# Hybrid streaming encoder step: two gate tiles move from the attention steps' fillers to a thirteenth block-product pair

## The chip, the cores and the metric

One NeuronCore of a Trainium2 chip runs the whole program. The metric is the device time of one execution in microseconds (us), taken as the median of several executions.

Engines are named as in the profile: PE is TensorE (matrix products; PEld its weight loads), DVE is VectorE, ACT is ScalarE, POOL is GpSimd, SP is the queue that issues most DMAs. Each of them runs its own program in order, and waits on semaphores that the others raise.

## What is computed

One layer of a streaming encoder, for 1024 prompt tokens and 32 sample tokens, in float32:

```python
z = x @ w_in                       # 1024 x 6416: heads of all branches, and gl, the 3 x 1024 merge gates
A: GLA linear attention            # 4 heads, per-token recurrence, in blocks
B: sliding-window attention        # 8 query heads, 2 kv heads, with sinks and partial rotary
C: cross attention                 # 4 heads into 256 memory tokens
mix = (sig(g_a)*y_a + sig(g_b)*y_b + sig(g_c)*y_c) @ w_o
x = LN1(alpha*x + mix);  x = LN2(alpha*x + ConvFFN(x))
```

The change concerns only where some columns of `gl` (the gates' part of `x @ w_in`) are computed. `gl` has 3072 columns, that is 24 tiles of 128.

## The kernel before

**Precision.** Every float32 product is made of three matmuls: operands are split into a high part (ACT copies it, rounded) and a low part (DVE subtracts it from the original), and hi x hi, hi x lo, lo x hi are accumulated (`product`, L1277).

**Dense tiles.** 128 columns of a weight are one tile. All 1058 token columns are passed in three slices (`GROUPS`, 352, 352 and 354 wide), each with 8 row blocks of 128, so a tile is 24 units of three matmuls. A slice is evacuated by ACT, and a gate tile's slices are stored in the scratch tensor `gates` by SP.

**Block-product pairs.** In the first long stage the columns are made two tiles at a time by a 2 x 2 block scheme with seven products in place of eight (`z_product`, L1302, `z_pair`, L1340): 7 products x 4 row blocks x 3 matmuls, for two halves of the tokens (256 and 274 wide), that is 168 matmuls for a pair. There are `NZ = 12` pairs: seven for the scan branch's columns, five for gate tiles, which `Z_GATES` names by the first of two. While PE works on pair n, ACT and DVE split the weights of pair n+1, snapshot and combine the results (`z_window`, L2083 on ACT, L2778 on DVE), and SP loads weights and stores the two tiles (`z_load`, `z_keep`). Raw weights, result buffers and PSUM banks alternate by the parity of the pair. Pairs 0 and 1 are written out, pairs 2 to 9 are a loop of four turns, 10 and 11 are written out again (L1418 to L1422). POOL makes sums of other weights in this stage.

**Scan stage.** The GLA recurrence, nine tiles of tokens; PE's gaps are filled with 14 dense tiles.

**Attention steps.** Then 8 token tiles are taken in 24 steps, three for each (window attention for kv pair 0 and 1, then memory attention), and three more short ones for the sample tokens. The order is written out by hand on each engine. PE, in step k = 6i + j (`att_steps`, L1667):

1. fillers: `ATT_UNITS = 6` units of a dense gate tile (`gate_slice_b`, L1651); the first three steps have other work in their place
2. `turn_probs(k)`, L1596: 8 transposes of the probabilities into PSUM
3. `scores(k+2)`, L1576 or L1581
4. `values(k)`, L1608 or L1613: needs prob_T, the transposed probabilities, copied back by DVE (one half) and ACT (the other)

DVE, in the same step (`att_steps`, L3005): its copy of prob_T(k) (L2980), `normalise(k+1)` (L2963: sum, reciprocal, four scalings L2974), `max_unit(k+2)` (L2939: mask add L2947, row maximum L2952, bias L2954; for memory units only the maximum L2959 and the bias L2961). In steps with j = 1 or 4 the copy of prob_T stands behind `normalise`. ACT (`att_steps`, L2291): an evacuation of a filler slice when one ends, its copy of prob_T(k) (L2236), the copy of the values (L2245), a split of the next weights when a tile ends, and `exp_unit(k+2)` (L2220), which waits for the bias from DVE; `normalise(k+2)` on DVE waits for it. Scores use the same PSUM banks each time, so `scores_read` (L1617) makes PE wait until they have been read. POOL copies the next token tile's operands when a memory unit's scores are made (`att_stage`, L1140).

With 24 units to a tile and six to a step, 24 steps (21 full ones and the three of the sample tokens) make six gate tiles, numbers 16 to 21, from turn `T_GATE_B`. In the sample steps (`r` = 0, 1, 2; from L1698 on PE, L2320 on ACT) ACT also makes the high parts of the branch outputs (`branch_hi`, L2317) for the merge stage, which begins with L1279 on `o_hi`.

**Queues and counts.** `gate_loop` (L845, SP) loads and stores the tiles of the attention steps; `load` waits until the slot's last weights were split. `T_MERGE`, `T_WO` and `T_FFN` number the weight tiles that follow, `PS_END` counts dense slices, `W0` counts loads.

Of the kernel before, what the change touches and what calls it, by code (L numbers as in the profile page):

```python
# [27 lines left out]
SEQ, DEC = 1024, 32  # L28
# [5 lines left out]
NT = SEQ // P  # L34
# [13 lines left out]
Z_BASE = (0, TT - 2 * HALF[1])  # L48
Z_FIRST = (0, 3, 1, 2, 5, 4, 6)
Z_SUMS = (1, 2, 4, 6)  # L50
NZ = 12
Z_LAST = (NZ - 1) % 2
ZA, ZS, ZC = NZ * 7, NZ * 4, NZ * 3
A_KEEP, Z_KEEP = 24, 34
FILL_ROWS = (0, 1, 8, 9, 2, 3, 4, 5)
NFILL = 14
FILL_SLICES = (5, 5, 5, 5, 5, 5, 4, 4, 4)
Z_GATES = (12, 14, 6, 8, 22)
ATT_UNITS = 6
H = 4  # L60
RANK = 16
GA_ROWS = 6 * RANK + 2
# [20 lines left out]
T_MQ = T_FILL + NFILL  # L83
# [1 line left out]
T_MQ_B = T_MQ + 3  # L85
T_MV = T_MQ + 6
T_GATE_B = T_MQ + 10
T_MERGE = T_MQ + 16
T_WO = T_MQ + 28
T_FFN = T_MQ + 36  # L90


PW0, PW1, PBG, PW2, PCB, PGN, PHI = 0, NF * 2, NF * 4, NF * 4 + 24, NF * 6 + 24, NF * 8 + 24, NF * 8 + 25
# [121 lines left out]
def program(nc, I, O, ctx):  # L215
# [114 lines left out]
    gate_st2 = [a.take(f"gate_stb{i}", [P, GW], F32) for i in range(3)]  # L330
# [175 lines left out]

    BRANCHES = (2, 0, 1)

    PS_Z, PS_G, PS_GA, PS_FILL, PS_MQ, PS_MQ_B, PS_MK, PS_MV, PS_GATE_B, PS_END = 6, 9, 11, 15, 57, 60, 63, 65, 67, 85
    q = Semaphores(sem)  # L510
    w_landed = [sem(f"w_landed{i}") for i in range(2)]
    x_landed = [sem(f"x_landed{i}") for i in range(6)]
    gate_stored = [sem(f"gate_stored{i}") for i in range(3)]
# [66 lines left out]
    LAST = NF - 1  # L580
# [4 lines left out]
    XH0, XL0, XS0 = 26, 17, 8  # L585
    HH0, HL0, XT0 = XH0 + len(X_ORDER), XL0 + len(X_ORDER), XS0 + 8
    D0 = T_FFN
    W0 = T_WO // 2 + 7
    KEPT = 16 * 9

    def mix_bank(p):
# [12 lines left out]
    def raw_count(c, par):  # L604

        if par:
            return 448 if isinstance(c, int) and c < 2 else c * 32 + 416
        return 32 * (W0 + 1) if isinstance(c, int) and c < 2 else c * 16 + 32 * (W0 + 1)

# [17 lines left out]
    d_landed = [w_landed[0], w_landed[1], h_landed[0], h_landed[1], rot_landed[0], rot_landed[1]]  # L627
    D_BASE = (32 * (W0 + NF // 2), 32 * (W0 + NF // 2), 0, 0, 16 * 8, 16 * 25)
    b_landed = [raw_b_landed, gate_landed[0], gate_landed[1], gate_stored[0], gate_stored[1], gate_stored[2]]
    B_BASE = (raw_count(LAST, 1), 192, 192, 16 * (8 + NFILL), 16 * (8 + NFILL), 16 * (8 + NFILL))  # L630
    B_RAWS = (1, 2, 1, 2, 1, 0, 0, 1, 1)

    def d_of(n):
# [56 lines left out]
    def _(sp):  # L690
# [154 lines left out]
        def gate_loop(turn0, chunk0, n, staging, stored0):  # L845

            for j in range(2):
                cols(turn0, j, w_in, C_GL + (chunk0 + j) * P)
            def stores(i, slots=(0, 1)):
                for j in slots:  # L850
                    for s, (c, w) in enumerate(GROUPS):

                        sp.wait_ge(q.proj_free, stored0 + i * 6 + 3 * j + s + 1)
                        sp.dma_start(gates[bass.ds(i * 2 + chunk0 + j, 1), :, c:c + w].rearrange("a p c -> p (a c)"),
                                     staging[s][:, 0:w]).then_inc(gate_stored[s], 16)
            with sp.Fori(0, n - 1) as i:
                for j in range(2):
                    cols(i + (turn0 + 1), j, w_in, i * 256 + C_GL + (chunk0 + 2 + j) * P)
                stores(i)
            return stores  # L860
# [36 lines left out]
        sp.dma_start(mask_first[:, :], I["c_mask_first"]).then_inc(q.params, 16)  # L897
        for n_ in range(4, 8):
            mem_tile(n_)
        last = gate_loop(T_GATE_B // 2, 16, 3, gate_st2, PS_GATE_B)  # L900


        def merge_tile(turn, slot, br, mp):
# [20 lines left out]

        merge_tile(T_MERGE // 2, 0, BRANCHES[0], 0)
        merge_tile(T_MERGE // 2, 1, BRANCHES[1], 0)
        last(2, (0,))
        sp.wait_ge(q.staged, 2 * NT + 2)
        sp.wait_ge(q.sample_turned, 1)
        gate_back(0)  # L930
        last(2, (1,))
        for s in range(3):
            sp.wait_ge(gate_stored[s], 16 * (8 + NFILL))

        for k in range(12):
            if k == 11:
# [339 lines left out]
    def _(pe):  # L1276
# [63 lines left out]
        def z_pair(n, par, j0=0):  # L1340
            for j in range(j0, NA):
                for s in range(2):
                    z_product(n, par, s, j)
# [71 lines left out]
        z_product(0, 0, 1, 6)  # L1415
        z_product(1, 1, 1, 0)
        z_pair(1, 1, 1)
        with pe.Fori(1, (NZ - 1) // 2) as i:  # L1418
            z_pair(i * 2, 0)
            z_pair(i * 2 + 1, 1)  # L1420
        z_pair(NZ - 2, 0)
        z_pair(NZ - 1, Z_LAST)  # L1422

        tile_start(1, 0)
# [165 lines left out]
        def turn_probs(k, par, w, widths):  # L1590
            pe.wait_ge(q.prob_ready, k + 1)
            pe.wait_ge(q.pT_dve, k)
            pe.wait_ge(q.pT_act, k)
            for h in range(H):
                for s, n in enumerate(widths):
                    last = pe.transpose(pair8(4)[0:n, 2 * h + s, 0:w], prob[par][0:w, h, s * P:s * P + n], ident[0:w, 0:w])  # L1596
            last.then_inc(q.prob_turned, 1)
# [53 lines left out]
        def gate_slice_b(i, j, beside=None):  # L1651

            for n_, (s, k) in enumerate(att_units(i, j)):
                slot, (c, w) = s // 3 % 2, GROUPS[s % 3]
                out = bank((PS_GATE_B + s) % 2)[:, 0:w]
                if k == 0:
                    if s % 3 == 0:
                        tile_start((T_GATE_B + s // 3) // 2, slot)
                    pe.wait_ge(q.proj_free, PS_GATE_B + s - 1)
                last = product(out, w_hi[slot][:, k, :], w_lo[slot][:, k, :], act_hi[:, k, c:c + w], act_lo[:, k, c:c + w],  # L1660
                               k == 0, k == KD - 1)
                if k == KD - 1:
                    last.then_inc(q.proj_done, 1)
                if beside and n_ in beside:
                    beside[n_]()
# [32 lines left out]
        for r in range(3):  # L1698
            k, widths = 3 * NT + r, (P, DEC) if r < 2 else (P, P)
            if r == 0:  # L1700
                gate_slice_b(NT // 2, r)
                turn_probs(k, k % 2, DEC, widths)
                sample_scores(2)
            else:
                gate_slice_b(NT // 2, r, {3: lambda: turn_probs(k, k % 2, DEC, widths)})
            pe.wait_ge(q.vt_ready, NT + 1)
            values(k, r, DEC, (v_hist, vt[0]) if r < 2 else mv[1], widths)

# [243 lines left out]
    def _(act):  # L1952
        def split_hi(turn, slot, dst=None, used=None):


            if used is not None:
                act.wait_ge(*used)
            act.wait_ge(w_landed[slot], 32 if isinstance(turn, int) and turn == 0 else (turn + 7) * 32)
            dst = w_hi[slot] if dst is None else dst
            act.activation(dst[:, :, :], w_raw[slot][:, :, :], ACT.Copy).then_inc(q.w_split_hi, 1)  # L1960

# [121 lines left out]
        def z_window(n, par):  # L2083
            for k in range(3):
                for s in range(2):
                    z_snap(n, par, s, k)
                z_split(n + 1, 1 - par, k)
            for j in (3, 4, 5):
                z_split(n + 1, 1 - par, j)
            for s in range(2):  # L2090
                z_snap(n, par, s, 3)
            z_split(n + 1, 1 - par, 6)

        z_window(1, 1)
        with act.Fori(1, (NZ - 1) // 2) as i:
            z_window(i * 2, 0)
            z_window(i * 2 + 1, 1)
        z_window(NZ - 2, 0)
        for k in range(3):
            for s in range(2):  # L2100
                z_snap(NZ - 1, Z_LAST, s, k)
# [23 lines left out]
        for gi, (c, w) in enumerate(GROUPS):  # L2125
            s = PS_GA + gi
# [232 lines left out]
        act.wait_ge(q.st_memv, 16)  # L2359
        act.wait_ge(q.v_out_ready, 1)  # L2360
        for gi in range(3):
            act.wait_ge(gate_stored[gi], 16 * (8 + NFILL))
        act.wait_ge(q.k_turned, 1)
        for place in range(3, 6):
            branch_hi(place)
# [300 lines left out]
    def _(dve):  # L2666
# [125 lines left out]
            z_low(n + 1, 1 - par, 6)  # L2792

        z_window(1, 1)
        with dve.Fori(1, (NZ - 1) // 2) as i:
            z_window(i * 2, 0)
            z_window(i * 2 + 1, 1)
        z_window(NZ - 2, 0)
        for k in range(3):
            for s in range(2):  # L2800
                z_combine(NZ - 1, Z_LAST, s, k)
# [681 lines left out]
```

## Time and profile before

| | us |
|---|---|
| median of 3 runs | 1712.73 (1712.61 to 1715.02) |
| the profiled execution, its own time | 1714.32 |
| its span, first to last instruction | 1712.5 |
| PE busy | 1689.7 (99%) |
| DVE busy | 1154.3 (67%) |
| ACT busy | 775.7 (45%) |
| POOL busy | 307.0 (18%) |

The stages by the timeline: block pairs from 42 to 291 us of the span, the scan stage to about 538, the memory keys and values and the first attention steps to 603, attention steps with fillers to 745, sample steps to 759, merging to about 906, output projection and layer norm to about 1010, the feed-forward to the end. A busy share is a mean over stages: whether an engine bounds a stage is read from its windows, waits and order of instructions.

### The profile page before, as it was taken

What the parts mean: (1) busy time and instruction counts of PE and PEld (TensorE: products, weight loads), DVE (VectorE), ACT (ScalarE), POOL (GpSimd) and SP (SyncE); (2) the same over time, 40 slices, a digit from 0 to 9 for tenths busy, and PEclk for the clock granted to TensorE, in tenths of its full rate; (3) what the DMA queues carried; (4) which work ended last, traced back from release to release, by engine and by line L of the source; (5) the groups of instructions that cost most, each with busy time, mean ns of one, the idle gap of its engine ahead of it and who ended that gap; (6) DMA issues with size and microseconds to landing.
All of it is one profiled execution on the core that took longest, in us unless ns stands there. A gap on an engine that the chain in (4) does not pass through costs nothing.

```text
span 1712.5 us, 32762 instructions
## 1 busy us (share of the span) xinstructions
PE 1689.7 (99%) x12447; PEld 1633.1 (95%) x12447; DVE 1154.3 (67%) x1687; ACT 775.7 (45%) x1500; POOL 307.0 (18%) x398
## 2 busy tenths in 40 slices
PE   9999999999999999999999999999999999999997
PEld 9999999999999889889997889999999999999997
DVE  6756553456673777667656698777777777777676
ACT  6433332354453555563332155455445445544562
POOL 0144342000010110000000004333333332000022
PEclk9999999999999999999999999999999999999999
DMA  5565665822154521124456332222222222787633
GB/s 169 162 223 199 211 216 169 278 76 76 59 166 126 170 81 47 43 65 150 137 177 218 108 96 79 75 74 74 75 82 85 80 74 88 271 302 247 207 102 100
DMA packets 196314, 232.75 MB, mean 136 GB/s; under 512 B 21973, under 2 KB 145430, under 8 KB 196214
## 3 DMA queue, kind: packets, MB, share of 16 engines
q1 hardware_dynamic: 188006, 201.66, 37.7%
q0 software_dynamic: 8208, 29.72, 4.8%
q8 instruction: 67, 1.10, 0.3%
q14 instruction: 33, 0.27, 0.0%
HBM read 170.69 MB, written 60.07 MB: 135 GB/s over the span
## 4 chain that ended last, share of the span: by engine, by line
PE 62%; DVE 5%; ACT 2%; issue 1%; POOL 0%; DMA 0%; DVEq 0%; ACTq 0%; POOLq 0%
PE banks L1836 24%; PE banks L1891 13%; PE banks L1279 5%; PE banks L1281 5%; PE banks L1280 5%; PE banks L1769 4%; PE banks L1596 1%; PE banks L1608 1%; PE banks L1613 1%; PE banks L1576 1%; ACT prob L2225 1%; PE banks L1581 1%; DVE prob L2974 1%; DVE wo L3050 0%; PE banks L1867 0%
## 5 line engine op out<-in xcount | busy, mean ns | idle before, releaser
L1836 PE MATMUL banks<-x_free_r,a_hi 128*128 128x256 f32 x1232 | 226.7, 282 | 2.0 <-DVE a_lo L3161 1.6
L1279 PE MATMUL banks<-act_hi,w_hi 128*128 128x352 f32 (+1 forms) x608 | 202.9, 334 | 0.0
L1281 PE MATMUL banks<-act_hi,w_lo 128*128 128x352 f32 (+1 forms) x608 | 197.8, 325 | 0.0
L1280 PE MATMUL banks<-act_lo,w_hi 128*128 128x352 f32 (+1 forms) x608 | 197.7, 325 | 0.0
L1836 PEld LDWEIGHTS banks<-x_free_r,a_hi 128*128 128x128 f32 x1232 | 190.1, 188 | 2.7 <-issue 1.2
L1836 PE MATMUL banks<-xs_hi,a_hi 128*128 128x274 f32 x616 | 178.8, 290 | 1.6 <-DVE xs_lo L3187 0.9
L1836 PE MATMUL banks<-xs_lo,a_hi 128*128 128x274 f32 x616 | 178.4, 290 | 0.0
L1836 PE MATMUL banks<-xs_hi,a_lo 128*128 128x274 f32 x616 | 178.3, 289 | 0.0
L1891 PE MATMUL banks<-b_hi,d_hi 128*128 128x238 f32 (+1 forms) x616 | 177.5, 288 | 0.4 <-DVE b_lo L3317 0.3
L1891 PE MATMUL banks<-b_hi,d_lo 128*128 128x238 f32 (+1 forms) x616 | 176.6, 287 | 0.0
L1891 PE MATMUL banks<-b_lo,d_hi 128*128 128x238 f32 (+1 forms) x616 | 176.4, 286 | 0.0
L1836 PE MATMUL banks<-x_free_r,a_lo 128*128 128x256 f32 x616 | 173.4, 281 | 0.0
L1836 PEld LDWEIGHTS banks<-xs_hi,a_hi 128*128 128x128 f32 x616 | 116.4, 189 | 2.2 <-DVE xs_lo L3187 1.4
L1891 PEld LDWEIGHTS banks<-b_hi,d_hi 128*128 128x128 f32 x616 | 116.9, 190 | 0.8 <-DVE d_lo L3284 0.5
L1279 PEld LDWEIGHTS banks<-act_hi,w_hi 128*128 128x128 f32 x608 | 115.1, 189 | 2.8 <-issue 2.4
L1891 PEld LDWEIGHTS banks<-b_lo,d_hi 128*128 128x128 f32 x616 | 117.2, 190 | 0.0
L1891 PEld LDWEIGHTS banks<-b_hi,d_lo 128*128 128x128 f32 x616 | 116.9, 190 | 0.0
L1836 PEld LDWEIGHTS banks<-xs_lo,a_hi 128*128 128x128 f32 x616 | 116.8, 190 | 0.0
L1836 PEld LDWEIGHTS banks<-x_free_r,a_lo 128*128 128x128 f32 x616 | 116.6, 189 | 0.0
L1836 PEld LDWEIGHTS banks<-xs_hi,a_lo 128*128 128x128 f32 x616 | 116.3, 189 | 0.0
L1280 PEld LDWEIGHTS banks<-act_lo,w_hi 128*128 128x128 f32 x608 | 115.2, 189 | 0.0
L1281 PEld LDWEIGHTS banks<-act_hi,w_lo 128*128 128x128 f32 x608 | 115.1, 189 | 0.0
(371 smaller groups left out, 4442.9 us busy)
## 6 DMA issues: line engine op xcount, KB each, us to landing
b_raw<-h_keep SPq DMA_DIRECT2D x77, 265.0 KB, 4.3
w_raw<-in_w_in SPq DMA_DIRECT2D x76, 256.0 KB, 3.9
gates_scratch<-zu SPq DMA_DIRECT2D x12, 1058.0 KB, 7.7
gate_in<-gates_scratch SPq DMA_DIRECT2D x24, 529.0 KB, 3.7
h_keep<-conv SPq DMA_DIRECT2D x22, 530.0 KB, 2.8
s_buf<-in_w_down POOLq DMA_DIRECT2D x11, 1024.0 KB, 5.3
s_keep<-s_buf POOLq DMA_DIRECT2D x22, 512.0 KB, 6.2
w_raw<-in_w_up SPq DMA_DIRECT2D x44, 256.0 KB, 3.9
```

The source lines that it names most:

```text
L1279: pe.matmul(out, hi, b_hi, start=start, stop=False)
L1280: pe.matmul(out, hi, b_lo, start=False, stop=False)
L1281: return pe.matmul(out, lo, b_hi, start=False, stop=stop)
L1576: last = pe.matmul(psum[0:w, 2 + r, h * 256:h * 256 + nk], qs[b][rows_, 2 * u + h, 0:w], keys[rows_, 0:nk], start=True, stop=True)
L1581: last = pe.matmul(out, mqs[b][:, h, 0:w], mkT[mem][:, h, :], start=True, stop=True)
L1596: last = pe.transpose(pair8(4)[0:n, 2 * h + s, 0:w], prob[par][0:w, h, s * P:s * P + n], ident[0:w, 0:w])
L1608: last = pe.matmul(bank4(6)[64 * r:64 * r + 64, h, 0:w], pair_[s][0:n, 64 * r:64 * r + 64], prob_T[0:n, 2 * (2 * r + h) + s, 0:w], start=( ...
L1613: last = pe.matmul(bank4(6)[:, h, 0:w], pair_[:, s, h * P:(h + 1) * P], prob_T[0:n, 2 * h + s, 0:w], start=(s == 0), stop=(s == 1))
L1769: last = pe.matmul(bank(b + half), x[:, k, c:c + P], w[:, place, 512 * half:512 * half + 512], start=k == 0 and n_ == 0, stop=k == KD - 1 ...
L1836: last = pe.matmul(out, a[j][:, k, :], x[s][j][:, k, :], start=fresh and k == 0 and n_ == 0, stop=k == 3 and n_ == 2, skip_group_check=True)
L1891: last = pe.matmul(out, x[d][:, mm * P:(mm + 1) * P], y[b][:, c - c0:c - c0 + w], start=fresh and n_ == 0, stop=stop and n_ == 2, skip_gro ...
L2225: last = act.activation(prob[par][0:w, h, 0:nk], src, ACT.Exp, bias=nbias[par][0:w, h:h + 1], scale=SWA_SCALE if r < 2 else MEM_SCALE, acc ...
```

## The change

The gate tiles 20 and 21 are made by a thirteenth block-product pair. The attention steps make four gate tiles instead of six, with four filler units in a step. The counts follow: the loop of pairs makes five turns (pairs 2 to 11), pair 12, of the other parity, is written out behind it, weight turns and PSUM slice counts behind the steps fall by two tiles, and in the second and third sample step the transposes come after the second filler unit instead of after the fourth.

```diff
-NZ = 12
+NZ = 13
-Z_GATES = (12, 14, 6, 8, 22)
-ATT_UNITS = 6
+Z_GATES = (12, 14, 6, 8, 22, 20)
+ATT_UNITS = 4
...
-T_MERGE = T_MQ + 16
-T_WO = T_MQ + 28
-T_FFN = T_MQ + 36
+T_MERGE = T_MQ + 14
+T_WO = T_MQ + 26
+T_FFN = T_MQ + 34
...
-    PS_Z, PS_G, PS_GA, PS_FILL, PS_MQ, PS_MQ_B, PS_MK, PS_MV, PS_GATE_B, PS_END = 6, 9, 11, 15, 57, 60, 63, 65, 67, 85
+    PS_Z, PS_G, PS_GA, PS_FILL, PS_MQ, PS_MQ_B, PS_MK, PS_MV, PS_GATE_B, PS_END = 6, 9, 11, 15, 57, 60, 63, 65, 67, 79
...
-    W0 = T_WO // 2 + 7
+    W0 = T_WO // 2 + 8
...
-        last = gate_loop(T_GATE_B // 2, 16, 3, gate_st2, PS_GATE_B)
+        last = gate_loop(T_GATE_B // 2, 16, 2, gate_st2, PS_GATE_B)
...
-        with pe.Fori(1, (NZ - 1) // 2) as i:
+        with pe.Fori(1, NZ // 2) as i:
             z_pair(i * 2, 0)
             z_pair(i * 2 + 1, 1)
-        z_pair(NZ - 2, 0)
         z_pair(NZ - 1, Z_LAST)
...
-                gate_slice_b(NT // 2, r, {3: lambda: turn_probs(k, k % 2, DEC, widths)})
+                gate_slice_b(NT // 2, r, {1: lambda: turn_probs(k, k % 2, DEC, widths)})
```

The loops of `z_window` on ACT and DVE change as that of `z_pair`, the waits for stored gate slices fall from `16 * (8 + NFILL)` to `16 * (6 + NFILL)`, and `split_hi` waits for a load count that is one higher.

## Rows read from the trace of the kernel before

**Rows 1.** The profile page, busy time of each engine (share of the span).

```profile
PE 1689.7 (99%) x12447; PEld 1633.1 (95%) x12447; DVE 1154.3 (67%) x1687; ACT 775.7 (45%) x1500; POOL 307.0 (18%) x398
```

**Rows 2.** Windows: length, then busy us (instructions) of PE, PEld, DVE, ACT, POOL, clock, DMA.

```profile
105.46:126.11 20.65, 20.65 (x170) 20.65 (x169) 11.56 (x17) 7.12 (x15) 8.43 (x7) 1.00 0.70 239
532.20:535.64 3.44, 3.44 (x14) 3.44 (x13) 0.99 (x5) 0.28 (x1) 0.79 (x1) 0.50 0.26 79
644.75:664.68 19.93, 19.85 (x153) 17.81 (x152) 14.26 (x31) 11.27 (x37) 1.90 (x4) 1.00 0.26 72
745.09:759.19 14.10, 13.78 (x119) 11.54 (x119) 9.21 (x19) 7.82 (x19) 1.35 (x3) 1.00 0.10 35
```

**Rows 3.** Waits from 602 to 746 us: total, times, longest.

```profile
DVE prob_T L2980 <- PE banks L1596: 28.9, 14, 3.0
...
DVE srec L2971 <- ACT prob L2225: 11.2, 7, 2.0
```

**Rows 4.** Timeline of DVE, three attention steps.

```profile
640.94 1.22 DVE L2947 TENSOR_TENSOR prob<-banks,mask 128x1024 f32<-128x1024 f32 x1
...
645.82 0.69 DVE L2980 COPY prob_T<-banks 128x512 f32<-128x512 f32 x1 [2.02 <-PE banks L1596]
646.43 0.15 DVE L2969 TENSOR_TENSOR sden<-ssum,sexp 128x4 f32<-128x4 f32 x1
...
646.83 1.14 DVE L2974 TENSOR_SCALAR prob<-prob,srec 128x256 f32<-128x256 f32 x4
647.89 1.22 DVE L2959 TENSOR_REDUCE smax<-banks 128x4 f32<-128x1024 f32 x1
649.14 0.47 DVE L2961 TENSOR_SCALAR nbias<-smax 128x4 f32<-128x4 f32 x1
651.60 0.18 DVE L2971 RECIPROCAL srec<-ssum 128x4 f32<-128x4 f32 x1 [2.00 <-ACT prob L2225]
...
652.88 0.68 DVE L2980 COPY prob_T<-banks 128x512 f32<-128x512 f32 x1
653.63 1.22 DVE L2947 TENSOR_TENSOR prob<-banks,mask 128x1024 f32<-128x1024 f32 x1
...
660.87 1.22 DVE L2947 TENSOR_TENSOR prob<-banks,mask 128x1024 f32<-128x1024 f32 x1
```

**Rows 5.** Timeline of ACT, the same steps.

```profile
643.64 0.51 ACT L2225 ACTIVATE prob<-prob,nbias 128x256 f32<-128x256 f32 x1 [1.01 <-DVE nbias L2954]
...
645.63 0.19 ACT L2230 ACTIVATE sexp<-sdif 128x4 f32<-128x4 f32 x1
...
649.64 0.47 ACT L2225 ACTIVATE prob<-banks,nbias 128x256 f32<-128x256 f32 x1 [0.67 <-DVE nbias L2961]
```

**Rows 6.** Timeline of PE: start, us, instructions: a transpose, and fillers.

```profile
602.88 1.04 PE L1596 MATMUL banks<-ident,prob 128*128 128x128 f32 x8
...
628.98 0.33 PE L1279 MATMUL banks<-act_hi,w_hi 128*128 128x352 f32 x1
...
630.93 0.32 PE L1279 MATMUL banks<-act_hi,w_hi 128*128 128x352 f32 x1
```

**Rows 7.** Timeline of DVE and POOL, 599 to 608 us.

```profile
600.16 2.33 DVE L2974 TENSOR_SCALAR prob<-prob,srec 128x256 f32<-128x256 f32 x4
...
606.68 1.60 DVE L2974 TENSOR_SCALAR prob<-prob,srec 128x256 f32<-128x256 f32 x4
...
600.62 0.71 POOL L1175 DMA_DIRECT2D mv_s<-in_cache_mem_v  x1
```

**Rows 8.** Timeline of ACT and PE, the sample steps.

```profile
750.77 1.36 ACT L2317 ACTIVATE o_hi<-z 128x1408 fp32r<-128x1408 f32 x1
...
753.72 2.65 ACT L2317 ACTIVATE o_hi<-z 128x1408 fp32r<-128x1408 f32 x2
...
752.54 0.31 PE L1608 MATMUL banks<-prob_T,v_hist 128*64 128x32 f32 x4 [0.32 <-ACT prob_T L2236]
...
757.32 1.87 PE L1613 MATMUL banks<-prob_T,mv_s 128*128 128x32 f32 x16
```

More of the change, by code:

```diff
@@ L629, in program @@
     b_landed = [raw_b_landed, gate_landed[0], gate_landed[1], gate_stored[0], gate_stored[1], gate_stored[2]]
-    B_BASE = (raw_count(LAST, 1), 192, 192, 16 * (8 + NFILL), 16 * (8 + NFILL), 16 * (8 + NFILL))
+    B_BASE = (raw_count(LAST, 1), 192, 192, 16 * (6 + NFILL), 16 * (6 + NFILL), 16 * (6 + NFILL))
     B_RAWS = (1, 2, 1, 2, 1, 0, 0, 1, 1)
@@ L926, in _ @@
         merge_tile(T_MERGE // 2, 1, BRANCHES[1], 0)
-        last(2, (0,))
+        last(1, (0,))
         sp.wait_ge(q.staged, 2 * NT + 2)
@@ L930, in _ @@
         gate_back(0)
-        last(2, (1,))
+        last(1, (1,))
         for s in range(3):
-            sp.wait_ge(gate_stored[s], 16 * (8 + NFILL))
+            sp.wait_ge(gate_stored[s], 16 * (6 + NFILL))
         for k in range(12):
@@ L1957, in split_hi @@
                 act.wait_ge(*used)
-            act.wait_ge(w_landed[slot], 32 if isinstance(turn, int) and turn == 0 else (turn + 7) * 32)
+            act.wait_ge(w_landed[slot], 32 if isinstance(turn, int) and turn == 0 else (turn + 8) * 32)
             dst = w_hi[slot] if dst is None else dst
@@ L2094, in _ @@
         z_window(1, 1)
-        with act.Fori(1, (NZ - 1) // 2) as i:
+        with act.Fori(1, NZ // 2) as i:
             z_window(i * 2, 0)
             z_window(i * 2 + 1, 1)
-        z_window(NZ - 2, 0)
         for k in range(3):
@@ L2361, in _ @@
         for gi in range(3):
-            act.wait_ge(gate_stored[gi], 16 * (8 + NFILL))
+            act.wait_ge(gate_stored[gi], 16 * (6 + NFILL))
         act.wait_ge(q.k_turned, 1)
@@ L2794, in _ @@
         z_window(1, 1)
-        with dve.Fori(1, (NZ - 1) // 2) as i:
+        with dve.Fori(1, NZ // 2) as i:
             z_window(i * 2, 0)
             z_window(i * 2 + 1, 1)
-        z_window(NZ - 2, 0)
         for k in range(3):
```

## The prediction

> **What bounds the kernel now.** I read the page first. TensorE (PE) is busy for 1689.7 of 1712.5 us [rows 1], so work taken from it should shorten the kernel, as long as nothing else is close behind. The question is what is close behind in the two stages that the change touches.
>
> The table of windows answers for the first. One pair of the block-product stage takes 20.65 us with PE busy for all of it, while VectorE (DVE) is busy 11.56 us and ScalarE (ACT) 7.12 us [rows 2]. A thirteenth pair will cost its matmuls and nothing more or less.
>
> For the attention stage the same table shows PE busy 19.85 of 19.93 us for three steps, DVE 14.26 and ACT 11.27 [rows 2]. By shares, DVE has room. But DVE and ACT take turns here, each waiting for the other, so their shares say little, and the timelines have to be read as a loop. On DVE, step k does normalise(k+1) and then max_unit(k+2); ACT does exp_unit(k+2) only after that maximum; and the next step's normalise(k+2) waits for that exponential. So every step holds one round: maximum (DVE), exponential (ACT), normalise (DVE), and only then the next maximum. In the table of waits DVE stood 28.9 us for the transpose of PE (14 times) but already 11.2 us, 7 times, for ACT's exponential [rows 3]: once in every three steps the round, not PE, was what DVE last waited for.
>
> **The round, priced.** A window-attention unit: mask add at 640.94, exponential at 643.64 (2.70 us); the sink's exponential begins 645.63 and ends 0.19 later, at 645.82 (2.18); sum, reciprocal and scaling run from 646.43 to the next instruction at 647.89 (1.46) [rows 4, 5]. That is 6.34, with about 0.03 for the hand-over back. A memory unit: reduce at 647.89, exponential at 649.64 (1.75), whose end releases the reciprocal at 651.60 (1.96), next instruction at 652.88 (1.28), and here the copy of prob_T stands behind the normalising and ahead of the next maximum, 652.88 to 653.63 (0.75) [rows 4, 5]: 5.74. Three steps hold two of the first kind and one of the second: 6.37 + 5.74 + 6.37 = **18.48 us**. They take 19.93 now (mask add 640.94 to mask add 660.87) [rows 4]. So the round lies only 1.45 us behind PE per three steps.
>
> **The change part by part.**
> *Thirteenth pair, added:* 168 matmuls on all-busy PE, 20.65 us [rows 2]. Its DVE, ACT and DMA work (one more set of splits, loads and stores) is like that of the pair before it, beside which both have over 9 us free; without that cover it would cost DVE's 11.6 us. Taken: **+20.65**, and I see nothing that could hide it. Another parity for the last pair, another semaphore count and one more turn of the loop in place of written-out code: nothing on PE, since it ran the same 20.65 in the loop, and the bank waits behind the last pair are covered by three dense slices.
>
> *Fillers, removed:* a filler unit is three matmuls; four of them go from 628.98 to 630.93, 0.4875 us each [rows 6]. Each of 24 steps loses two, 0.975 us; 48 units are 23.4 us of PE. If PE stayed the bound, the sum would be 20.65 - 23.4 = -2.75.
> It does not. Three steps would need 19.93 - 2.93 = 17.0 us of PE, while the round needs 18.48. What goes from the steps is then 1.45 us per three, and the other 1.48 comes back as waits of PE: ahead of values(k), whose prob_T copy stands behind the exponential in ACT's order, and ahead of the next scores. The 21 full steps that have fillers are seven threes: 7 x 1.45 = 10.2 us. The filler ahead of the first of them gives 0.3 more at most, since its transpose at 602.88 follows a normalising that ended 602.49 [rows 6, 7].
>
> *The three sample steps at the end* lose 2.9 us of fillers as well. But there PE already waited 0.32 for ACT at 752.54, because ACT's copy of prob_T stood behind a branch copy (1.36 us from 750.77); two more (2.65 us from 753.72) stand ahead of its last copy, whose values came at 757.32 [rows 8]. That line of ACT work starts from the scores of the first sample step, which do not move against their transpose. I give it 0.2. Two slot loads, six slices' stores and two splits fewer: queues that wait for PE, nothing. Merging onwards is the same work.
>
> **Sum.** 20.65 - 10.2 - 0.3 - 0.2 = +9.95 us. The profiled execution took 1714.32 (span 1712.5, 1.8 around it), which gives 1724.3; it stands 1.6 above the median of 1712.73, so the forecast for the median is **1722.7**.
>
> **Bounds of what the trace does not show.** How tightly the round runs when nothing else stops it: the memory unit's bias instruction at 649.14, on four numbers a row, took 0.47 [rows 4]; if it took a third of that, and half of the 0.75 copy fell beside another wait, three steps would come to about 17.8 and save 15.4 in all: 1718.0. From the other side, normalising takes 1.14 alone, but 1.60 and 2.33 where it ran beside POOL's copies [rows 4, 7]. POOL copies the next tile when the memory scores end. Now that is just as normalising finishes; with PE running ahead of the round it is sooner against it. At +0.46 for six tiles this adds 2.8: 1725.5. And the clock: the granted clock fell to 0.50 (1.2 GHz) once before the end, from 532.20 for 3.4 us, with 14 matmuls in that window [rows 2]; at a filler's 0.1625 each [rows 6] they would have taken 2.3 us, so 1.2 us was lost. The steps will have less PE work; two such falls would add 2.4: 1727.9. Nearest is the round as it ran in the rows above, so I keep it and carry the ends to the range: 1718 to 1728.
>
> **Rivals.**
> *PE stays the bound (the other side).* The round could be shorter than I add up, if some wait in it is only there because PE came late. It must fall under 17.0 us per three steps for PE to keep everything: then it is -2.75, or about 0 where the sample steps still give nothing: 1710.0 to 1712.7, not slower. For it: DVE waited 28.9 us for PE in this stage. Against it: those waits lay mostly beside the exponential, which ended at the same 645.82 as the copy began [rows 4, 5]; and the order of DVE's instructions fixes the round. Chance 0.07, and 0.04 more for a half-way result between 1710 and 1716.
> *The round also collides with POOL.* If each tile's normalising is slowed as at 600.16 (2.33 instead of 1.14 [rows 4, 7]), six times 1.19 is 7.1 more: 1729.8. For it: POOL's copies start on the very scores that PE now delivers early. Against: half of the 2.33 lay beside DMA issues of POOL, the last of which ended at 601.33 [rows 7], and they do not recur. Chance 0.12.
> The Trainium skill (SBUF — State Buffer, Who interferes with whom) says that a tensor_scalar of DVE and a GpSimd instruction take a shared port pair as an exclusive lock, the later one blocked for the whole of the other. By that rule the result would be this rival's; the trace agrees that DVE is held up, with 0.46 and 1.19 more [rows 4, 7], and no row here shows a meeting in which it is held for all the copies.
> *Clock falls often.* PE would wait some 0.5 us in every step beside small matmuls; if the clock fell in each of seven threes, 7 x 1.2 = 8.4 more, part of it beside the waits: about 1727 to 1731. Chance 0.05.
> The Trainium skill (TensorE: Matmul & The Clock Gate, HAM oscillation) tells of kernels in which waits of PE between bursts bring the slow clock again and again. [...]
> *The change does not do what it says:* only if the two tiles were still done in the steps; the constants leave 96 units for 4 tiles, so no.
>
> **How the numbers follow.** My case has 0.72, the collision 0.12, the clock 0.05, PE as the bound 0.07, half-way 0.04. The last two are the only ones not slower. A measurement of this kernel tells about 0.2% (3.4 us) from no change, so slower begins at 1716.2 and faster ends at 1709.3, which even the best case here does not reach: slower 0.89, same 0.09, and 0.02 for faster, for what I overlook. The range 1717.5 to 1728.0 holds my case with its bounds and the low side of the collision.
>
> **What would show it.** Right: a thirteenth 20.65 us in the block stage; three attention steps between 18 and 19 us, PE's wait ahead of the values matmuls and ahead of scores for the first time each step, on DVE and ACT prob_T and on the exponential; DVE's 28.9 us behind PE's transpose mostly gone and its wait for ACT grown; the stretch from the first sample transpose to the first merge matmul still about 14 us. Wrong: three steps at 17 us (the round was slack), or near 20 (collisions), or a granted clock under 1.00 in the steps.

## The result and the profile after

The changed kernel takes 1729.55 us, the median of five runs (1727.27 to 1732.33), beside 1713.94 for the kernel before in the same five rounds (1712.61 to 1715.02). The ratio is 1.0091 with an interval of 1.0080 to 1.0102: **slower by 15.6 us**. The profiled execution took 1732.33, the longest of the five, and its span is 1730.5. One execution of the kernel before, beside the first four experiments, took 4237 us, and the ratios leave it out.

To see where the time went I cut both spans at the same places of the program (first and one of the last matmuls of the block products, first transposes of steps 0, 3 and 24, first merge matmul, first matmul of the output projection and of the feed-forward). The fillers of a step stand ahead of its transposes, so "steps 3 to 23" holds the fillers of steps 4 to 24, and those of the first sample step are among them. The second profile of the changed kernel is that of `after_again`, below.

| stage, us | before | after | after_again |
|---|---|---|---|
| block-product pairs | 249.03 | 269.67 | 269.67 |
| scan stage, memory keys, up to step 0 | 292.31 | 293.29 | 290.73 |
| steps 0 to 2 | 19.53 | 19.20 | 19.20 |
| steps 3 to 23 | 142.22 | 132.05 | 132.02 |
| sample steps, up to the first merge matmul | 14.10 | 16.96 | 16.25 |
| merging | 140.47 | 142.80 | 141.97 |
| output projection, layer norm | 103.18 | 104.34 | 103.32 |
| whole span | 1712.50 | 1730.52 | 1724.81 |

The pair costs 20.64, the steps give back 10.2 and 0.3, and the feed-forward differs by 0.4 at most. But the sample steps and the merging, where I had forecast -0.2, cost 5.2 in the one profile and 3.7 in the other.

The windows of the changed kernel (start:end, length, then busy us of PE, PEld, DVE, ACT, POOL, granted clock, DMA share, GB/s): a block pair, two times three attention steps, the sample steps in two parts, the first merge matmuls, and the merging from there on.

```profile
291.16:311.83 20.67, 20.67 (x170) 20.67 (x169) 4.42 (x9) 4.59 (x10) 0.00 (x0) 1.00 0.47 131
644.61:663.51 18.90, 17.11 (x134) 15.00 (x133) 13.44 (x31) 10.89 (x37) 1.95 (x4) 1.00 0.06 20
663.50:682.00 18.50, 17.04 (x136) 14.97 (x134) 14.30 (x31) 9.58 (x35) 1.96 (x4) 1.00 0.03 11
756.40:764.84 8.44, 7.14 (x70) 5.18 (x69) 5.82 (x16) 4.84 (x18) 0.00 (x0) 1.00 0.07 24
764.84:773.33 8.49, 8.49 (x39) 7.97 (x39) 3.61 (x4) 3.60 (x6) 1.60 (x4) 0.50 0.10 31
773.33:778.49 5.16, 5.16 (x20) 5.16 (x19) 1.75 (x2) 5.13 (x6) 0.00 (x0) 0.50 0.31 105
778.49:916.00 137.51, 137.51 (x848) 137.51 (x848) 87.28 (x137) 52.75 (x50) 1.07 (x2) 1.00 0.50 145
```

Beside [rows 2]: three steps fell from 19.93 to 18.5 or 18.9, and PE, which had been busy for all but 0.08 of them, now idles 1.5 to 1.8 in these threes. The seven threes are not alike: from step 3 on they took 21.8, 20.1, 19.9, 19.9, 20.9, 20.1 and 19.6 before, and 20.3, 18.9, 18.5, 18.9, 19.5, 18.2 and 17.8 after, so each saved between 1.0 and 1.8, where the forecast had 1.45 for every one. And the granted clock, which was 1.00 through the sample steps and the merging of before, is at 0.50 (1.2 GHz) from 764.84 to 778.49, for 13.65 us. In the lines of that part PE is "busy" throughout: a slow clock shows as busy time, not as a wait.

The waits of the changed kernel from 624 to 757 us (total, times, longest):

```profile
DVE prob_T L2977 <- PE banks L1595: 17.1, 11, 2.3
DVE srec L2968 <- ACT prob L2223: 14.0, 7, 2.0
...
PE banks L1607 <- DVE prob_T L2977: 4.4, 5, 1.2
PE banks L1575 <- ACT prob L2223: 2.5, 6, 0.8
...
PE banks L1612 <- ACT vt L2249: 2.0, 6, 0.5
PE banks L1607 <- ACT prob_T L2234: 1.8, 3, 1.4
```

The 28.9 us in which DVE waited for PE [rows 3] are down to 17.1, its wait for the exponential is up from 11.2 to 14.0, and PE now waits ahead of the values matmuls for the copies of DVE and ACT, and ahead of the scores for the exponential, as the forecast said.

The round itself, in the timeline of DVE (start, duration, instruction, idle before it), one line for each place where the forecast had a term:

```profile
641.64 1.22 DVE L2944 TENSOR_TENSOR prob<-banks,mask 128x1024 f32<-128x1024 f32 x1
...
646.62 0.16 DVE L2966 TENSOR_TENSOR sden<-ssum,sexp 128x4 f32<-128x4 f32 x1 [0.25 <-ACT sexp L2228]
...
647.04 1.50 DVE L2971 TENSOR_SCALAR prob<-prob,srec 128x256 f32<-128x256 f32 x4
648.45 1.21 DVE L2956 TENSOR_REDUCE smax<-banks 128x4 f32<-128x1024 f32 x1
649.70 0.17 DVE L2958 TENSOR_SCALAR nbias<-smax 128x4 f32<-128x4 f32 x1
...
653.13 0.69 DVE L2977 COPY prob_T<-banks 128x512 f32<-128x512 f32 x1
653.73 1.22 DVE L2944 TENSOR_TENSOR prob<-banks,mask 128x1024 f32<-128x1024 f32 x1
...
660.18 1.22 DVE L2944 TENSOR_TENSOR prob<-banks,mask 128x1024 f32<-128x1024 f32 x1
```

Window unit 641.64 to 648.45: 6.81 (6.37 forecast), of which 0.36 is the normalising that ran 1.50 beside POOL's copy of the next tile instead of 1.14. Memory unit 648.45 to 653.73: 5.28 (5.74 forecast); its bias took 0.17 and not 0.47, which is 0.30 of the 0.46. Window unit to 660.18: 6.45. The sum is 18.54, the forecast 18.48; it is right in the sum, with two terms off by over 0.4 in opposite directions, and that they cancel is luck.

The sample steps, in the timeline of PE:

```profile
763.83 0.31 PE L1607 MATMUL banks<-prob_T,v_hist 128*64 128x32 f32 x4 [1.30 <-ACT prob_T L2234]
...
764.78 0.64 PE L1279 MATMUL banks<-act_hi,w_hi 128*128 128x354 f32 x1
765.21 0.50 PE L1280 MATMUL banks<-act_lo,w_hi 128*128 128x354 f32 x1
765.50 0.50 PE L1281 MATMUL banks<-act_hi,w_lo 128*128 128x354 f32 x1
...
769.74 3.46 PE L1612 MATMUL banks<-prob_T,mv_s 128*128 128x32 f32 x16
...
773.33 0.64 PE L1279 MATMUL banks<-o_hi,w_hi 128*128 128x352 f32 x1
773.77 0.49 PE L1280 MATMUL banks<-z_lo,w_hi 128*128 128x352 f32 x1
774.07 0.49 PE L1281 MATMUL banks<-o_hi,w_lo 128*128 128x352 f32 x1
```

The wait of 0.32 at this place [rows 8] has become 1.30, as two removed units ought to make it. Behind it the clock falls. The last values matmuls take 3.46 instead of 1.87 [rows 8]; matmuls that followed each other every 0.1625 [rows 6] are 0.295 apart, and the merging starts in that state too. By these two distances its 5.16 us at 0.50 hold work of 5.16 x 0.1625 / 0.295 = 2.84, which is 2.3 lost (an estimate), just what the merging lost (142.80 against 140.47).

### The profile page after: what moved, and what is told of

It reads as the page before. It is cut to its first block, busy times and chain, and to the rows that moved or that the text cites. A ratio compares the mean times of both kernels' runs of the same rounds, so it can differ in the third digit from the quotient of the medians.

```text
span 1730.5 us, 32846 instructions
## 1 busy us (share of the span) xinstructions
PE 1694.9 (98%) x12471; PEld 1636.7 (95%) x12471; DVE 1167.2 (67%) x1702; ACT 776.8 (45%) x1507; POOL 305.1 (18%) x398
## 4 chain that ended last, share of the span: by engine, by line
PE 56%; DVE 6%; ACT 3%; issue 1%; DMA 1%; SPq 1%; DVEq 0%; POOL 0%; ACTq 0%; POOLq 0%
PE banks L1835 25%; PE banks L1890 13%; PE banks L1768 4%; PE banks L1279 4%; PE banks L1280 3%; PE banks L1281 3%; ACT prob L2223 2%; DVE prob L2971 1%; PE banks L1612 1%; DMA kpad<-gates_scratch 1%; DVE smax L2956 1%; DVE smax L2949 0%; DVE wo L3047 0%; PE banks L1866 0%; PE banks L1595 0%
## 5 line engine op out<-in xcount | busy, mean ns | idle before, releaser
L1279 PE MATMUL banks<-act_hi,w_hi 128*128 128x352 f32 (+1 forms) x560 | 188.0, 336 | 0.0
L1281 PE MATMUL banks<-act_hi,w_lo 128*128 128x352 f32 (+1 forms) x560 | 183.0, 327 | 0.0
L1280 PE MATMUL banks<-act_lo,w_hi 128*128 128x352 f32 (+1 forms) x560 | 182.9, 327 | 0.0
L1336 PE MATMUL banks<-zt_hi,za_hi 128*128 128x256 f32 (+1 forms) x416 | 118.6, 285 | 1.0 <-DVE za_lo L2715 1.0
L1336 PE MATMUL banks<-zt_lo,za_hi 128*128 128x256 f32 (+1 forms) x416 | 118.4, 285 | 0.0
L1336 PE MATMUL banks<-zt_hi,za_lo 128*128 128x256 f32 (+1 forms) x416 | 118.4, 285 | 0.0
```

Source lines behind the costliest of these rows:

```text
L1279: pe.matmul(out, hi, b_hi, start=start, stop=False)
L1280: pe.matmul(out, hi, b_lo, start=False, stop=False)
L1281: return pe.matmul(out, lo, b_hi, start=False, stop=stop)
L1336: last = pe.matmul(bank(b)[:, 0:w], a[j][:, k, :], v[:, k, :], start=fresh and k == 0 and n_ == 0, stop=k == 3 and n_ == 2, skip_group_che ...
```

## The experiments

The theory behind the forecast: PE pays the pair in full, and the steps stop at the round of DVE and ACT. Rivals: the steps are held by something else (meetings with POOL, clock); the loss in the sample steps is a wait of the new order, not the clock.

### The two halves alone, and a shorter round

`pair_only` has the thirteenth pair but keeps six filler units and three pairs of tiles in the steps, so that tiles 20 and 21 are made twice:

```diff
-ATT_UNITS = 4
+ATT_UNITS = 6
-        last = gate_loop(T_GATE_B // 2, 16, 2, gate_st2, PS_GATE_B)
+        last = gate_loop(T_GATE_B // 2, 16, 3, gate_st2, PS_GATE_B)
```

> The thirteenth pair is added and the steps keep their six fillers, so tiles 20 and 21 are made twice. Theory A (the pair costs its matmuls, and what the forecast missed lies at the end of the attention steps): 20.7 us over the kernel before, ratio 1.012, and the sample steps and the merge at full clock as before. Rival B (the pair costs more than its matmuls, by what it shifts between the block stage and the steps, and in the output projection: the 1.1 and 1.2 us found there): 22 to 23.5 us, ratio above 1.013.

Measured: 1732.63, ratio 1.0113 (1.0097 to 1.0130) to 1714.61. In its profile the pairs take 269.65, and the steps and the merging are as before: 142.09 for steps 3 to 23, 14.10 for the sample steps, 140.47 for merging. **The pair is 20.6 us of plain PE time** and disturbs neither. The whole kernel is only 18.0 over by the medians and 18.1 by the two profiles, under the 20.7 expected: the profile of `pair_only` has no fall of the clock in its scan stage, which is 1.5 shorter than that of before, and its first block product begins 0.6 sooner.

`fill4_only` is the other half: twelve pairs, four filler units. Tiles 20 and 21 are not computed; the merging reads tiles 18 and 19 in their place.

```diff
-ATT_UNITS = 6
+ATT_UNITS = 4
...
-                sp.dma_start(gate_in[j][:, :], gates[k % 3 * KD + k // 3 * 2 + j])
+                row = k % 3 * KD + k // 3 * 2 + j
+                sp.dma_start(gate_in[j][:, :], gates[row - 2 if 20 <= row < 22 else row])
```

> Four fillers in a step and no thirteenth pair; tiles 20 and 21 are left out, and the merge reads tiles 18 and 19 in their place. Theory A: the 21 steps save 10 us (18.4 to 18.9 for three), the sample steps and the first merge matmuls lose 3 to 6 by a halved clock, so 4 to 7 us under the kernel before, ratio 0.996 to 0.9975. Rival C (the loss at the end was a chance of the one profile): 10 to 11 us under, 0.994. Rival D (PE bounds the steps): 23 us under, 0.986.

Measured: 1707.8, ratio 0.9962 (0.9948 to 0.9976). Of 23.4 us of PE work taken out, 6.8 arrive, inside the 4 to 7 expected. The steps give 10.2 (132.06), the sample steps and the merging take back 3.3 + 1.7 (17.42, 142.20), with the clock at 0.50 for 13.65 us from 743.35. So both effects belong to the thinner steps and neither to the pair.

`after_short` and `before_short` shorten the round and leave PE's work alone: DVE takes the row maximum over keys 128 to 191 only (the other 192 are not looked at, so the softmax is shifted by another number). `after_short`:

```diff
-                dve.tensor_reduce(smax[par][0:w, :], dst, AX_X, ALU.max)
+                dve.tensor_reduce(smax[par][0:w, :], dst[:, :, P:P + 64] if nk == 2 * P else dst, AX_X, ALU.max)
...
-                dve.tensor_reduce(smax[par][0:w, :], scores4[0:w, :, 0:nk], AX_X, ALU.max)
+                dve.tensor_reduce(smax[par][0:w, :], scores4[0:w, :, P:P + 64], AX_X, ALU.max)
```

> The changed kernel, with the row maximum of DVE taken over 64 of the 256 keys in both kinds of unit (the bias of the softmax is then another; nothing else is left out). The round maximum, exponential, normalise is 0.9 us shorter in each step; the work of PE is the same. Theory A (the round bounds the steps): three steps fall from 18.5 or 18.9 to 17.0 to 17.6, the 21 steps by 7 to 9 us, the kernel to 1720 to 1723, ratio to the kernel before 1.004 to 1.006. Rival D (PE bounds the steps, and fillers are simply worth less than counted): no change against the changed kernel, ratio 1.009.

> The kernel before with the same shorter maximum. Theory A: PE bounds these steps, three of them stay at 19.7 to 19.9 and the kernel within 2 us of the kernel before, ratio 0.999 to 1.0. A rival by which DVE's work itself is on the path in both kernels: 5 to 9 us less, 0.995 to 0.997.

Measured: `after_short` 1718.91, ratio 1.0022 (1.0010 to 1.0033); `before_short` 1712.13, ratio 0.9990 (0.9980 to 0.9999). Three steps of `after_short`, then of `before_short` (columns as above):

```profile
641.86:659.06 17.20, 16.95 (x134) 14.93 (x133) 10.50 (x31) 10.22 (x35) 1.81 (x4) 1.00 0.07 22
```

```profile
642.85:662.62 19.77, 19.77 (x154) 17.78 (x152) 11.75 (x31) 11.16 (x38) 1.91 (x4) 1.00 0.26 73
```

The same edit takes 8.7 us from steps 3 to 23 of the changed kernel (132.05 to 123.33) and 1.7 from those of before (142.22 to 140.49). With the short maximum three steps take 17.20, and the forecast had put PE's need at 17.0. **The round is the bound after the change, and PE was the bound before it**, but for the first three steps with fillers: of the 1.7 us, 1.2 come from these (21.79 to 20.58), where PE had stood idle already in the kernel before:

```profile
602.88:624.67 21.79, 19.88 (x152) 17.82 (x151) 15.55 (x34) 11.21 (x40) 2.12 (x5) 1.00 0.25 81
```

In the profile of `after_short` the sample steps still take 16.69 and the merging 142.74, the clock is at 0.50 from 754.54 for 13.65 us: a shorter round does not cure that part. This is the longest of its eight executions, 1721.42 at a mean clock of 0.993. The shortest took 1715.89 at 0.997, a mean clock that the kernel before and `tail_dummy` (below), whose profiles have no fall in the sample steps, show too. So the fall may have been shorter or missing in some of them, which would be why the median lies under the 1720 to 1723 expected.

### The sample steps

`after_again` is the changed kernel once more, to see which of its losses come again.

> The changed kernel itself once more, beside the others of this call. Theory A: 13 to 16 us over the kernel before, the clock at half for 6.8 to 13.7 us about the end of the attention steps again. The 1.1 us more ahead of the steps and the 1.2 us more in the output projection that its first profile showed are a chance of that execution and are gone or elsewhere.

Measured: 1728.73, ratio 1.0090 (1.0073 to 1.0106). The stage table above has its profile. The 1.0 us ahead of the steps and the 1.2 in the output projection of the first profile are gone, and so is a fall of 3.41 us in the scan stage, which the kernel before had too [rows 2]; it comes in some executions of each. The fall in the sample steps is there again:

```profile
753.68:763.00 9.32, 8.02 (x75) 6.05 (x74) 6.06 (x16) 5.68 (x20) 0.00 (x0) 1.00 0.06 22
763.00:773.24 10.24, 10.24 (x45) 9.73 (x45) 4.59 (x4) 5.98 (x8) 1.94 (x4) 0.50 0.24 79
```

In all nine executions of the changed kernel the mean clock was 0.993 to 0.995, in those of before 0.996 to 0.998.

`tail_dummy` adds work to the changed kernel: in each sample step PE makes two idle units, six matmuls of 352 columns into the PSUM bank that nobody reads at the time, ahead of the transposes in the first two steps and ahead of the values in the third.

```diff
+        def idle_units(r, n):
+            pe.wait_ge(q.proj_free, PS_GATE_B + (10, 11, 11)[r])
+            out = bank((PS_GATE_B + (11, 10, 10)[r]) % 2)
+            for u in range(n):
+                product(out[:, 0:352], w_hi[1][:, u, :], w_lo[1][:, u, :], act_hi[:, u, 0:352], act_lo[:, u, 0:352], True, True)
...
+            if r < 2:
+                idle_units(r, 2)
...
+            if r == 2:
+                idle_units(r, 2)
```

> The changed kernel with two units of matmuls more in each sample step, whose results go to a PSUM bank that nobody reads: 18 matmuls more, 2.9 us of PE at full clock, nothing else changed. Theory A (PE's small load about the sample steps halves the clock): more matmuls make it faster, sample steps 14.1 to 14.6 against 17.0, merge 140.5 against 142.8, 4 to 5 us under the changed kernel. Rival C: the sample steps take as long or 1 to 3 us longer, the kernel 0 to 3 us over the changed kernel.

Measured: 1725.58, ratio 1.0067 (1.0050 to 1.0084). **Eighteen matmuls more, and the kernel is about 3.2 us faster** than `after_again`, measured beside it; all four executions of the one (1725.17 to 1725.71) lie under all four of the other (1726.62 to 1730.72). Expected were 4 to 5; of what is missing, 0.9 are the first two idle units, which PE makes ahead of the transposes of step 24, where no wait takes them up. The sample steps and the merging of `tail_dummy`:

```profile
756.11:770.21 14.10, 13.78 (x119) 11.55 (x119) 9.34 (x19) 7.66 (x18) 1.65 (x4) 1.00 0.09 32
770.21:910.68 140.47, 140.47 (x866) 140.47 (x865) 90.02 (x141) 58.03 (x55) 1.07 (x2) 1.00 0.49 146
```

This is [rows 2] again, to the hundredth: 14.10, PE busy 13.78, clock 1.00.

`tail6` tries the same with useful work: three filler units in six of the full steps, four in the others, six in the sample steps.

```diff
+UNITS = [3 if m in (3, 6, 9, 12, 15, 18) else 4 for m in range(21)] + [6, 6, 6]
...
-        first = (6 * i + j - 3) * ATT_UNITS
-        return [divmod(u, KD) for u in range(first, first + ATT_UNITS)]
+        m = 6 * i + j - 3
+        first = sum(UNITS[:m]) if m >= 0 else -KD
+        return [divmod(u, KD) for u in range(first, first + UNITS[max(m, 0)])]
```

> The changed kernel with its 96 filler units dealt out otherwise: six in each of the three sample steps, as before the change, three in six of the full steps, four in the other fifteen. The same work in all. Theory A (the round bounds the full steps, so that fillers there are free to leave; the sample steps lose by the halved clock): full steps as in the changed kernel (130.5 to 133 us from the first with fillers to the first sample step), sample steps back to 14.1 and the merge to 140.5 at full clock, 4 to 6 us under the changed kernel, ratio to the kernel before 1.0055 to 1.007. Rival C (the halved clock is not tied to the fillers of the sample steps): as the changed kernel, 1.009.

Measured: 1726.36, ratio 1.0072 (1.0055 to 1.0088), sample steps 14.10, merging 140.47, clock 1.00 in both. It is 2.4 us under `after_again`, less than the 4 to 6 expected, and the executions of the two overlap (1725.72 to 1727.27 against 1726.62 to 1730.72). The full steps took 133.91, 1.9 more than with four units everywhere. About 1.1 of this lies at the end of the stretch: the last three has 18.9 instead of 17.8, since the two fillers more of the first sample step stand ahead of the transposes of step 24. And two threes went to 19.5 and 20.5, a microsecond over the changed kernel's. In both the normalising ran 2.12 instead of 1.50, because POOL's copies now began with it and not 0.6 us later; DVE, then POOL, in the first of them:

```profile
664.82 2.12 DVE L2974 TENSOR_SCALAR prob<-prob,srec 128x256 f32<-128x256 f32 x4
```

```profile
664.86 0.61 POOL L1148 COPY qs<-z 128x512 f32 x1 [16.61 <-PE banks L1583]
665.42 0.46 POOL L1150 COPY ks<-kpad 128x256 f32 x1
665.82 0.35 POOL L1153 COPY vs<-z 128x128 f32 x1
666.12 0.67 POOL L1156 COPY mqs<-z 128x512 f32 x1
```

That is the mechanism of the prediction's collision rival: scores that PE delivers earlier start the copies sooner against the normalising. It did not come in the changed kernel, and one filler less in a step brings part of it: 0.62 in each of the two threes. Where the other 0.4 of each comes from is open.

`fill2_only` takes out two more units in every step (tiles 18 to 21 are not computed; the merging reads tiles 16 and 17 in their place), to see whether PE's work counts at all any more.

> Two fillers in a step, no thirteenth pair; four gate tiles are left out (the merge reads tiles 16 and 17 for them). Theory A (the round bounds the full steps from four fillers on): three steps take 17.6 to 18.8 us as with four, though PE has 2.9 us less to do; the 21 steps 130 to 132 us against 132.1 with four and 142.2 with six; the halved clock covers more of the stage, which may add 2 to 5. Kernel 1702 to 1711. Rival D (PE or a cost per filler bounds them still): 15.6 us for three steps or less, 112 for the 21, the kernel about 1688.

Measured: 1710.76, ratio 0.9983 (0.9973 to 0.9992): it has 23.4 us less to do on PE than `fill4_only` and is not faster for it: 1707.8 and 0.9962 there, and the two intervals just overlap (0.9976 and 0.9973). Steps 3 to 23 took 136.13, where I had expected 130 to 132, because the clock now falls inside them. Two stretches of its attention steps:

```profile
642.50:649.22 6.72, 3.88 (x37) 3.50 (x38) 4.47 (x12) 3.64 (x13) 1.80 (x4) 1.00 0.00 0
649.22:656.04 6.82, 6.28 (x35) 5.19 (x31) 3.77 (x7) 2.56 (x10) 0.00 (x0) 0.50 0.08 29
```

In the first, with PE busy 3.88 of 6.72 us, the clock is full; then it is half for 6.83 us. The same comes from 669.70 and from 690.18, and for 13.65 us in the sample steps. Less work for PE made PE the slow one. There is one more fall, of 3.41 us from 611.67, in the first three.

Since the clock falls in four of the seven threes, the sum of 136.13 does not by itself tell what the round does. The other three, the second, sixth and seventh, ran at full clock throughout:

```profile
620.49:639.62 19.13, 14.18 (x116) 12.08 (x115) 13.88 (x31) 9.59 (x34) 1.81 (x4) 1.00 0.03 10
702.59:719.91 17.32, 14.23 (x115) 12.14 (x116) 12.15 (x28) 9.42 (x34) 1.09 (x4) 1.00 0.22 73
719.91:737.02 17.11, 13.48 (x117) 11.29 (x114) 11.72 (x33) 9.54 (x35) 0.00 (x0) 1.00 0.04 13
```

The same threes of `fill4_only` took 18.89, 18.23 and 17.79. With 8.8 us less for PE these three gave back 1.35 in all, and PE idles 3 to 5 us in each: PE does not bound them, and rival D's 15.6 is not reached.

### The reverse, and both remedies

`before_tail4` is the kernel before with its fillers moved: 7 units in six of the full steps, 6 in the others, and only 4 in each sample step. All 24 tiles are made as before.

```diff
+UNITS = [7 if m in (2, 5, 8, 11, 14, 17) else 6 for m in range(21)] + [4, 4, 4]
...
-                gate_slice_b(NT // 2, r, {3: lambda: turn_probs(k, k % 2, DEC, widths)})
+                gate_slice_b(NT // 2, r, {1: lambda: turn_probs(k, k % 2, DEC, widths)})
```

> The kernel before, same 144 filler units, but four instead of six in each of the three sample steps; the six units that they lose go to six full steps (seven units there). No thirteenth pair, nothing else. Theory A (thin sample steps halve the clock by themselves): full steps 2.9 us longer, since PE bounds them; sample steps 16 to 17.5 us instead of 14.1 and the merge 141.5 to 143 instead of 140.5; 6 to 8 us over the kernel before, ratio 1.0035 to 1.005. Rival E (it takes thin full steps ahead of them as well): clock full, sample steps 13.9 to 14.1, 2.5 to 3 us over the kernel before, 1.0015 to 1.002.

Measured: 1719.96, ratio 1.0039 (1.0025 to 1.0053), +6.1 us with the same total of work. Steps 3 to 23 take 144.49 (2.3 more, for four more units, 1.95 us, in this stretch: six added to the full steps, two taken from the first sample step), the sample steps 15.84, the merging 142.46. Its sample steps, before and after the fall:

```profile
745.19:755.16 9.97, 8.67 (x81) 6.48 (x81) 6.06 (x16) 6.32 (x21) 0.00 (x0) 1.00 0.05 20
755.16:765.40 10.24, 10.24 (x44) 10.11 (x43) 4.99 (x5) 6.38 (x9) 2.35 (x4) 0.50 0.23 77
```

So the fall needs neither the pair nor the thin full steps, only the thin sample steps.

`short_dummy` is the changed kernel with the short maximum of `after_short` and the idle units of `tail_dummy`, to see how far the change gets with both its obstacles out of the way.

> The changed kernel with both remedies: the shorter row maximum (64 of 256 keys, so the softmax's bias differs) and the two idle units in each sample step. Theory A (two independent losses, the round and the clock): full steps 123 to 124 us as with the shorter maximum alone, sample steps at most 14.1 and the merge 140.5 at full clock, 4 us under the shorter maximum alone: 1714 to 1716, within 0.1% of the kernel before. Rival: the remedies overlap, and it stays at 1717 to 1719.

Measured: 1716.08, ratio 1.0015 (1.0005 to 1.0024) to 1713.82. Steps 3 to 23 take 124.21, the sample steps 13.73, the merging 140.47: the two remedies add up, stage by stage. It is still not under the kernel before, and just outside the 1714 to 1716 expected. What PE must do more (20.64 for the pair, 2.9 for the idle units) and less (23.4) leaves it nothing to win with.

## Why the prediction was wrong, and where it was right

- **Bound of the block stage, +20.65:** right. 20.62 to 20.64 in every profile with the pair.
- **The round as the bound, -10.2 in 21 steps and -0.3 ahead of them:** right, 10.17 and 0.33. The price of the round was 18.48, and in the three steps that I had priced it ran in 18.54. Shown to be the bound by the pair of short-maximum runs (-8.7 against -1.7), and by the threes of `fill2_only` at full clock, where 8.8 us less of PE work brought 1.35. That seven equal threes give the sum is in part luck: they saved from 1.0 to 1.8 each.
- **The bounds around it:** the memory bias took 0.17, as the lower bound had allowed. The normalising ran 1.50 instead of 1.14 at four token tiles, 1.4 us in all, half of the 2.8 that I gave the upper bound. The two about cancelled, which I had no ground to expect. The collision rival, six times 1.19, did not come: no normalising in steps 3 to 23 took longer than 1.50. It lay close by, though: in `tail6` two took 2.12.
- **The step that failed: the sample steps, "I give it 0.2", and "Merging onwards is the same work".** The work is the same, but not the clock it runs at. From 763 to 765 us PE drops to 1.2 GHz for 10.24 or 13.65 us, and the sample steps and merging cost 3.7 to 5.2 more than before instead of 0.2 less. I had noticed that the clock could fall, but I priced a fall with the only one in the trace, 1.2 us for 3.41 us of slow clock [rows 2], and looked for it in the full steps. Those kept 1.00. The price of a fall is its length and what work it covers: here dense merge matmuls, whose whole slow-down goes on the path. The clock rival had the mechanism with the wrong place and a chance of 0.05. The Trainium skill (TensorE: Matmul & The Clock Gate, HAM oscillation), named beside it, does not bear this rival out: its waits are longer than any at these falls. The 0.2 itself no run shows: at full clock two units fewer turned into a wait of 1.30 at the second step's values, 0.98 more, and the clock fell before the rest could be seen.
- **The sum without it:** `tail_dummy`, whose clock stays up, is 11.3 us over its kernel before. Its idle units add about 0.9 to the last full step (18.74 against 17.82 for the last three). That leaves 10.4, and the forecast was 9.95; the difference is under what these medians can tell. With the fall, 14.5 to 15.6 us.
- **My range** ended at 1728.0 and the median is 1729.55. It let two short falls stand at its end, added to nothing else. A fall of this length in the sample steps alone makes 1722.7 + 5.4 = 1728.1, and another 1.2 us is how far the median of before moved from three runs to five (1712.73 to 1713.94).

Not settled: what sets whether and where the clock falls. A three of `fill2_only` kept it with PE busy 14.18 of 19.13 us, the sample steps lost it with 7.14 of 8.44. Whether fewer than eighteen idle matmuls would hold it was not tried.

## What to carry to other kernels

When fillers are taken from a stage, ask two things of what remains: which loop between other engines is next behind PE (add up one turn of it from the timeline, since busy shares do not show it), and whether PE keeps its clock in the thinnest steps of the stage, which the granted clock of a run tells. Read the thinnest steps by themselves, and look at what dense stage follows, because that stage pays for the fall. If the change's best case is worth only 2.75 us of 1713, as here by PE's arithmetic, one such side effect decides it.

## What the runs showed of the hardware

The granted clock went to half where PE had never stood still for long. Ahead of the fall in the changed kernel PE was busy 7.14 of 8.44 us with one wait of 1.30 ahead of values matmuls of 32 columns; the rest were transposes, scores, values and four filler units. With six units in the same steps (busy 13.78 of 14.10) it stayed up, in `tail_dummy` with matmuls whose result nobody uses. Once half, it stayed there for 10.24 or 13.65 us, though PE was busy in all of it (8.49 of 8.49 and 5.16 of 5.16 in the changed kernel, with fillers, transposes, the values matmuls of 32 columns and, at the end, merge matmuls), and in the attention steps of `fill2_only` for 3.41 or 6.83. The full steps with four units idled 1.5 to 1.8 of 18.5 to 18.9 us, in waits of up to 1.4, and kept the full clock, and so did three steps of `fill2_only` that idled 4.95 of 19.13.

The Trainium skill (TensorE: Matmul & The Clock Gate, A second HAM failure mode: psum-queue depth-cycling) tells of a kernel in which short idle times of PE between groups of matmuls bring the slow clock again and again; the traces of `fill2_only` agree, with a half clock of 6.83 us from 649.22, 669.70 and 690.18. The same page (HAM oscillation) ties the slow clock to one gap of PE, longer than any at these falls: the longest wait ahead of the fall was 1.30 us here, and in `fill2_only` 2.10 in the full steps and 2.71 at the sample steps. So the measurement decides: the clock fell without such a gap. The length of one wait does not tell when, for full steps with waits of up to 1.4 us kept the clock.

The Trainium skill (SBUF — State Buffer, Who interferes with whom) has DVE and GpSimd share a pair of ports, which an instruction that takes it, as a tensor_scalar of DVE can, holds to its end while the other waits. The traces agree. In the changed kernel the four scalings began at 647.04 and took 1.50 instead of 1.14, and ended 0.15 after POOL's copy of 0.76 us from 647.63; only the last of the four was held, 0.70 instead of 0.35. In `tail6`, where the copies began with the scalings, each of the four ended 0.15 after one of POOL's four copies (at 665.62, 666.02, 666.32 and 666.93, the copies at 665.48, 665.88, 666.17 and 666.79), and they took 2.12. So what a meeting costs goes by how many of the copies the scalings meet: 0.36 for one, 0.98 for all four.
